# The rotary partners of the differential queries and keys, exchanged by SBUF-to-SBUF DMAs in place of TensorE's permutation products

## The reference, cut to what matters

```
q = rms_norm(x @ w_q, g_q);  k = rms_norm(x @ w_k, g_k)        # per head of 64 features
q = q * cos + partner(q) * sin;  k = k * cos + partner(k) * sin  # partner: feature d and d + 32 exchanged,
                                                               # the first half with a minus sign
p = softmax(q1 k1 / 8) - lambda * softmax(q2 k2 / 8);  out = p @ v   # 8 heads, each of two halves
```

## Time and profile before

| what | value |
|---|---|
| time, median of 3 runs | 1079.1 us (1078.55 to 1080.32) |
| time of the profiled execution | 1077.96 us |
| its span, first to last instruction | 1076.2 us |
| TensorE busy | 1042.4 us (97% of the span) |
| VectorE, ScalarE, GpSimd busy | 731.7, 552.9, 202.2 us |
| granted TensorE clock, mean | 0.995 |
| DMA: the core's queue of SyncE | 191.15 MB, 52.5% of 16 engines |
| the stretch of a slab in the queries and keys | 14.74 us |

### The profile page before, as it was taken

One profiled execution on the slowest core, in us unless ns is written; L12 is line 12 of the kernel. 1 busy time (PEld: TensorE's weight loads), 2 busy tenths in 40 slices (PEclk: granted clock), 3 DMA queues, 4 the chain that ended last, 5 costly groups with the idle time before them and its releaser, 6 DMA issues.

```text
span 1076.2 us, 20430 instructions
## 1 busy us (share of the span) xinstructions
PE 1042.4 (97%) x7993; PEld 981.9 (91%) x7993; DVE 731.7 (68%) x1155; ACT 552.9 (51%) x946; POOL 202.2 (19%) x223
## 2 busy tenths in 40 slices
PE   5999999999999999999999999999989999999998
PEld 5577788999999998989999999998877999999998
DVE  5798777767654788868556555686787765564565
ACT  2223457545363585527454444566467764544453
POOL 0000012233311001022333321021210223322010
PEclk9999999999999999999999999999999999999999
DMA  9993453577556454504564546654322265644661
GB/s 350 399 389 121 169 184 98 195 254 262 174 168 190 137 192 173 183 2 153 186 209 156 174 131 203 247 185 157 131 105 79 93 222 178 212 132 140 185 208 40
DMA packets 183587, 192.78 MB, mean 179 GB/s; under 512 B 5913, under 2 KB 143426, under 8 KB 183522
## 3 DMA queue, kind: packets, MB, share of 16 engines
q1 hardware_dynamic: 182512, 191.15, 52.5%
q0 software_dynamic: 144, 0.52, 0.2%
q10 hardware_dynamic: 866, 0.21, 0.1%
HBM read 190.83 MB, written 1.05 MB: 178 GB/s over the span
## 4 chain that ended last, share of the span: by engine, by line
PE 56%; DVE 5%; ACT 3%; issue 1%; POOL 0%; DVEq 0%; POOLq 0%; ACTq 0%
PE gemm L2219 17%; PE gemm L2221 17%; PE gemm L2220 16%; DVE wlo L1464 1%; PE aux L2717 1%; PE aux L2835 1%; PE aux L2767 1%; ACT whi L899 1%; DVE prod L1943 1%; PE gemm L2820 1%; PE aux L2773 0%; PE aux L2219 0%; DVE state L2075 0%; PE aux L2221 0%; PE aux L2220 0%
## 5 line engine op out<-in xcount | busy, mean ns | idle before, releaser
L2219 PE MATMUL gemm<-ohi,whi 128*128 128x256 f32 x1376 | 389.5, 283 | 3.8 <-issue 1.1
L1464 DVE TENSOR_TENSOR wlo<-raw,whi 128x1024 fp32r<-128x1024 f32 (+1 forms) x308 | 352.2, 1187 | 58.8 <-ACT whi L899 58.1
L2220 PE MATMUL gemm<-olo,whi 128*128 128x256 f32 x1376 | 385.8, 280 | 0.0
L2221 PE MATMUL gemm<-ohi,wlo 128*128 128x256 f32 x1376 | 383.6, 279 | 0.0
L899 ACT ACTIVATE whi<-raw 128x1024 fp32r<-128x1024 f32 (+1 forms) x308 | 276.4, 963 | 60.4 <-PE gemm L2221 44.2
L2219 PEld LDWEIGHTS gemm<-ohi,whi 128*128 128x128 f32 x1376 | 259.1, 188 | 6.7 <-DVE wlo L1464 2.8
L2220 PEld LDWEIGHTS gemm<-olo,whi 128*128 128x128 f32 x1376 | 259.5, 189 | 0.6 <-issue 0.5
L2221 PEld LDWEIGHTS gemm<-ohi,wlo 128*128 128x128 f32 x1376 | 259.4, 189 | 0.0
L2221 PE MATMUL gemm<-acthi,wlo 128*128 128x256 f32 x528 | 147.8, 280 | 0.0
L2219 PE MATMUL gemm<-acthi,whi 128*128 128x256 f32 x528 | 147.5, 279 | 0.0
L2220 PE MATMUL gemm<-actlo,whi 128*128 128x256 f32 x528 | 147.3, 279 | 0.0
(11 more groups left out here) (383 smaller groups left out, 1549.0 us busy)
## 6 DMA issues: line engine op xcount, KB each, us to landing
raw<-in_ffn_w_in SPq DMA_DIRECT2D x44, 1024.0 KB, 6.2
raw<-in_ffn_w_out SPq DMA_DIRECT2D x32, 704.0 KB, 5.2
part<-in_w_ada SPq DMA_DIRECT2D x32, 512.0 KB, 10.7
raw<-in_gla_w_in SPq DMA_DIRECT2D x6, 2048.0 KB, 7.8
raw<-in_diff_w_in SPq DMA_DIRECT2D x6, 2048.0 KB, 7.9
raw<-in_w_gate SPq DMA_DIRECT2D x11, 1024.0 KB, 6.3
raw<-in_w_up SPq DMA_DIRECT2D x11, 1024.0 KB, 8.5
raw<-in_w_down SPq DMA_DIRECT2D x16, 704.0 KB, 5.2
```

The source lines that it names most:

```text
L1464: dve.tensor_tensor(wlo[hslot][:, q * w:(q + 1) * w], src[:, q * w:(q + 1) * w], whi[hslot][:, q * w:(q + 1) * w].bitcast(F32), ALU.subtra ...
L2219: pe.matmul(dst, st_hi, mv_hi, start=start, stop=False)
L2220: pe.matmul(dst, st_hi, mv_lo, start=False, stop=False)
L2221: return pe.matmul(dst, st_lo, mv_hi, start=False, stop=stop_)
```

## The change

The `rot_d` matrix is no longer made or loaded, and the sign of the partner goes into the table `sin_d`. The partners of a pair are fetched by four DMAs of 32 partitions (32 x 2 KB, 64 KB each), which ScalarE issues: block b of 32 partitions is read from block b xor 1. They land in one of two SBUF buffers `d_rot`, which lie in the place of `ohi`. For each of the 4 DMAs the semaphore of the buffer rises by 16. ScalarE issues them for the two pairs of the stretch before in one go, in front of the third quarter (`ahead` comes before `after` at tile 0), and those of pairs 6 and 7 between the second and the third quarter of the values' slab. Before them it waits for the pair's `normalize` and, from pair 2 on, for the turn two pairs earlier. `turn` waits for the DMAs, multiplies by the sine in place and adds. The product `partners` is gone from TensorE's program, and with it the wait of `turn` for TensorE.

```
         if tag == "d":
+            sin *= rot.sum(0)[:, None]
...
+        d_t1 = sb("d_t1", 512, at=U + 10240)
+        d_rot = [sb(f"d_rot{i}", 512, at=place["ohi"] + 512 * i) for i in range(2)]
...
+            def move_partners(r):
+
+                src = tl(d_q, 2 * r, 2) if r < 4 else tl(d_k, 2 * r - 8, 2)
+                act.wait_ge(qk_normed, r + 1)
+                if r >= 2:
+                    act.wait_ge(qk_ready, r - 1)
+                for b in range(4):
+                    act.dma_start(d_rot[r % 2][32 * b:32 * b + 32, :], src[32 * (b ^ 1):32 * (b ^ 1) + 32, :]).then_inc(
+                        qk_moved[r % 2], 16)
+
             for base, name in ((0, "diff_q"), (4, "diff_k")):
                 def after(at, t, base=base):
                     buf = d_q if base == 0 else d_k
+                    if t == 0 and base + at.i:
+                        for r in (base + 2 * at.i - 2, base + 2 * at.i - 1):
+                            move_partners(r)
...
             for q in range(4):
                 ahead(*VALUES, q)
+                if q == 1:
+                    move_partners(6)
+                    move_partners(7)
             take_values(0)
...
             def turn(r):
-                me.next(qk_rot)
-                me.again(qk_ready)
-                me.did(dve.tensor_tensor(v3(d_t2[:, :], 2), v3(X[2 + r % 2][:, :], 2), bc(C("sin_d", T), 2), ALU.mult),
-                       qk_rot_read)
+                rot = d_rot[r % 2]
+                dve.wait_ge(qk_moved[r % 2], 64 * (r // 2 + 1))
+                me.did(dve.tensor_tensor(v3(rot[:, :], 2), v3(rot[:, :], 2), bc(C("sin_d", T), 2), ALU.mult), qk_turned)
                 me.next(qk_cos)
-                me.again(qk_rot_read)
-                me.did(dve.tensor_tensor(pair(r), d_t1[:, :], d_t2[:, :], ALU.add), qk_ready)
+                me.again(qk_turned)
+                me.did(dve.tensor_tensor(pair(r), d_t1[:, :], rot[:, :], ALU.add), qk_ready)
...
-            def partners(r):
-                banks.claim(X[2 + r % 2], qk_rot_read)
-                pe.wait_ge(qk_normed, r + 1)
-                src = tl(d_q, 2 * r, 2) if r < 4 else tl(d_k, 2 * r - 8, 2)
-                pe.matmul(X[2 + r % 2][:, :], C("rot_d"), src, start=True, stop=True).then_inc(qk_rot, 1)
...
-                    if t == 1 and r:
-                        partners(r - 2)
                     if t == 3:
-                        if r:
-                            partners(r - 1)
                         block_sums(r)
                         block_sums(r + 1)
...
-            value_steps(0, 8)
-            partners(6)
-            partners(7)
-            value_steps(8, 16)
+            value_steps(0, 16)
```

More of the change, by code:

```diff
@@ L77 @@
 CONSTS = [("ident", P), ("rot_q", P), ("rot_i", P), ("cos_q", T), ("sin_q", T), ("cos_i", T), ("sin_i", T),
-          ("causal", 3 * P), ("blk", P), ("rot_d", P), ("cos_d", T), ("sin_d", T), ("gla_mask", 2 * P)]
+          ("causal", 3 * P), ("blk", P), ("cos_d", T), ("sin_d", T), ("gla_mask", 2 * P)]
 COL_C, NC = column_of(CONSTS)
@@ L103, in shape_constants @@
                 cos[m], sin[m] = np.cos(ang[d % half]), np.sin(ang[d % half])
-        put("rot_" + tag, rot)
+        if tag == "d":
+            sin *= rot.sum(0)[:, None]
+        else:
+            put("rot_" + tag, rot)
         put("cos_" + tag, cos)
@@ L387, in build @@
         d_sq, d_rs = sb("d_sq", 1024, at=U + 8192), sb("d_rs", 1024, at=U + 9216)
-        d_t1, d_t2 = sb("d_t1", 512, at=U + 10240), sb("d_t2", 512, at=U + 10752)
+        d_t1 = sb("d_t1", 512, at=U + 10240)
+        d_rot = [sb(f"d_rot{i}", 512, at=place["ohi"] + 512 * i) for i in range(2)]
         d_nsq = sb("d_nsq", 2048, at=U)
@@ L452, in build @@
             sem("u_read"), sem("go_done"), sem("go_read"), sem("gated"))
-        qk_src, qk_sq, qk_stat, qk_sd, qk_normed, qk_cos, qk_rot, qk_rot_read, qk_ready = (
+        qk_src, qk_sq, qk_stat, qk_sd, qk_normed, qk_cos, qk_turned, qk_ready = (
             sem("qk_src"), sem("qk_sq"), sem("qk_stat"), sem("qk_sd"), sem("qk_normed"), sem("qk_cos"),
-            sem("qk_rot"), sem("qk_rot_read"), sem("qk_ready"))
+            sem("qk_turned"), sem("qk_ready"))
+        qk_moved = [sem("qk_moved0"), sem("qk_moved1")]
         out_done, out_read, last_read, stored = sem("out_done"), sem("out_read"), sem("last_read"), sem("stored")
```

## The result

The changed kernel takes 1082.04 us in the median of 11 runs (1080.64 to 1085.22), the kernel before in 11 runs beside it 1078.64 (1077.57 to 1080.87). The ratio is 1.0033 with a 95% interval of 1.0024 to 1.0042: 3.4 us slower by the medians, where 2.6 us faster was forecast. The range, 1074.6 to 1079.2, does not hold it. The profiled execution spans 1081.2 us against 1076.2.

The account below looks back on a forecast made before the run. TensorE was taken to bound the kernel up to pair 7's block sums, then a VectorE and GpSimd chain. 3.45 - 0.3 (issues) - 0.2 (pair 6) - 0.3 (clock) = 2.65 us, so 1079.1 becomes 1076.5; range 1074.6 to 1079.2.

Parts of the forecast that it names:

- TensorE is rid of 6.9 us, of which the pieces behind tile 3 turn into waits for the square: Eight partner products of 0.86 us leave TensorE; each of three query/key stretches gets 1.15 us shorter, 3.45 us in all.
- the cover that was forecast: In the stretches, VectorE's 1.33 us wait for tile 3 shrinks by 0.86, leaving 0.47 us to absorb lateness.
- I take 0.44 each, between, 3.5 us in all.: ScalarE's eight DMA issues a stretch, before quarter 2: quarter 2 0.3 to 0.4 us late, 0.3 us charged in total.
- Second rival: ScalarE's issues at 0.58 us make quarter 2 1.4 us late, costing 0.9 us a stretch; taken as 1078.0 us, chance 0.14.
- The DMAs land in time, 2.2 us: Partner DMAs of 64 KB land 2.2 us after issue, so everything up to pair 5 is hidden.
- The slower rival: DMAs land after 6.6 us, making turn(6) 4.0 us late and the stretches' turns 0.7; 1082.4 us, chance 0.07.
- 0.2 us charged for pair 6, nothing for pair 7: In the values, pair 6's DMAs land with 0.35 us over, less under a load's tail; pair 7's land in time.
- a gap of 1.9 us in TensorE: Before scores(1), TensorE stands from 787.5 to 789.4 waiting for take_values(0); the wait itself was taken as free.
- Clock, 0.3 charged: A clock fall in TensorE's new idle time before scores(1) would mostly use up the later 1.3 us wait; 0.3 us.
- the first rival: The clock falls in the new wait before scores(1) and lasts past 794.07: 1.7 us instead of 0.3, 1077.9 us, chance 0.18.
- Last rival: The slow clock near 805 us is absent after the shift, saving 1.7 us more: 1074.8 us, chance 0.08.
- The products of pairs 6 and 7 gain nothing: In the values, removing two products off the chain turns their 1.72 us of TensorE time into waiting.

Follow-up runs that it names:

- e1: Changed kernel with its partner DMAs issued by SyncE instead of ScalarE, in front of the following weight load; 1077.12 us, ratio 0.9988 to the kernel before.
- e6: Kernel before, all products kept, plus idle copies from ScalarE with the same bytes in 8 DMAs of 128 partitions; 1078.78 us, ratio 0.9996.
- e3: Changed kernel with TensorE's products back for pairs 0 to 5, ScalarE's DMAs only for pairs 6 and 7; 1078.09 us, ratio 1.0006.
- e9: Changed kernel with DMAs issued by SyncE, plus four unused TensorE products in front of scores(2); 1074.61 us, ratio 0.9966 to the kernel before.
- e2: Changed kernel with TensorE's products back for pairs 6 and 7, ScalarE's DMAs for pairs 0 to 5; 1080.66 us, ratio 1.0021.
- e10: Changed kernel with ScalarE's DMAs behind the fourth quarter for pairs 0 to 5, TensorE's products for pairs 6 and 7; 1075.07 us, ratio 0.9965.
- e5: Changed kernel with SyncE issuing the DMAs of pairs 0 to 5, TensorE's products for pairs 6 and 7; 1075.25 us, ratio 0.9967.
- e8: Changed kernel with ScalarE's 32 issues moved behind the fourth quarter instead of the second; 1077.13 us, ratio 0.9983 to the kernel before.
- e4: Kernel before, all products kept, plus 32 idle copies of 32 partitions issued by ScalarE at the changed kernel's places; 1081.75 us, ratio 1.0033.
- e7: Changed kernel with both pairs of a stretch in the same four DMAs, 16 issues instead of 32, from ScalarE; 1078.29 us, ratio 0.9999.

## Why the prediction was wrong, point by point

- *TensorE is rid of 6.9 us, of which the pieces behind tile 3 turn into waits for the square.* Right, once nothing else is in the way. The forecast stretch was 14.74 - 1.15 = 13.59; six versions show 13.67. In e1 VectorE waits 0.47 us for tile 3, the cover that was forecast:

```profile
763.14 0.42 DVE L2017 TENSOR_TENSOR d_k<-gemm,rstd 128x256 f32<-128x256 f32 x1 [0.47 <-PE gemm L2240]
```

- *"I take 0.44 each, between, 3.5 us in all."* **The step that failed.** An issue took 0.61 us, eight 5.0 to 6.0. The row called nearest in form, 0.49 for 128 partitions, was nearest to e6 (0.47 for 128 partitions) and not to a DMA of 32 partitions; the longest row, 0.58, would have come nearest. Quarter 2 came 1.88 us late instead of 0.35, and with 0.47 us of cover that is 1.41 of each stretch. The difference to 13.67 measured is 1.35. In the first stretch an issue of 1.47 us came on top, and the cover there was small, as forecast (0.10): quarter 2 was 2.84 us late and 2.67 were lost. The sum for the stretches was +2.16 us and not -3.1. The prediction had named issues above 0.5 us, and a clock below 1 between 788 and 800 us, as signs that it was wrong; both came.
- *Second rival, ScalarE's issues set the stretch.* The right mechanism, with its arithmetic (lateness less 0.47 of cover), but priced too low: it took 8 issues of 0.58, 4.6 us, where 5.0 to 6.0 were measured. It stood in the prediction as faster or no change; with 1.35 us lost a stretch and 2.67 in the first it crosses over.
- *The DMAs land in time, 2.2 us.* Right: 2.1 in the median. The slower rival, landing at 6.6 us, did not happen, although its 1082.4 is near the measured 1082.04; the time agreed by chance, and the turns of the stretches waited for no DMA. The 2.15 us that the prediction took from the Trainium skill ("DMA: Bandwidth & Descriptors", section "Anatomy of one DMA") is given there for DMAs that GpSimd issues; ScalarE's came out near it.
- *Values: 0.2 us charged for pair 6, nothing for pair 7.* Too low by the same term. Eight issues of 0.61 put the landing behind the turn's place and cost 0.7 us in e1 and e3. In the changed kernel one of the eight took 1.49 us, the last began at 791.70, and it was 1.52.
- *ScalarE's quarters end near 788.5 and `take_values(0)` at 789.4, which leaves a gap of 1.9 us in TensorE.* The place was right, the size not: 4.29 us, again by the issues. In e3, without the long issue, it was 3.40.
- *Clock, 0.3 charged, 1.7 as the first rival* (the text above the sum calls it the second). In the profile of the change it cost 1.69 us on the path; e9 against e1 shows 0.0022 of 1079, 2.4 us, for a wait of 3.77 us. What was held against this rival, that the new gap of 1.9 us is shorter than the one that brought a fall, is a misreading. TensorE was still at work until 802.66, and its wait before the fall was 1.91 us too:

```profile
804.57 1.78 PE L2820 MATMUL gemm<-d_k,d_q 64*128 64x256 f32 x8 [1.91 <-ACT d_p L1409]
```

That same wait of 1.91 us has a fall behind it in the kernel before, e2, e6 and e10, and none in the changed kernel and the other runs (e5 and e10 differ in this though TensorE has the same products and waits in both), and in e8 waits of 1.81 and 2.17 us passed without one. So a gap of 1.9 us can go either way. That the charge of 0.3 suits it was not tested by itself.
- *Last rival, the fall near 805 us is not there after the shift.* It was not there in the profile of the changed kernel, which took 1.7 us off the loss. As e5 and e10 show, it comes and goes without such a change, so no run ties it to this one.
- *The products of pairs 6 and 7 gain nothing.* Right, and more: e5 and e10 keep them and are the fastest versions without added work.

What stays open: why some single issues take 1.1 to 1.7 us (one in the first stretch of all eight runs that issue 32 x 2 KB DMAs there, one in the values of the changed kernel and of e4), and the mean price of the clock in the changed kernel, since each program has one profile and the mean clock of its runs differs (0.990 to 0.993).

## What to carry to other kernels

Work that leaves one engine as DMAs comes back on the issuing engine's sequencer: count the issues, multiply by a row of the same partition count, and ask what stands behind them in that engine's program. Here the same 32 issues, two quarters further down, turned a loss of 0.33% into a gain of 0.17%. And where an engine waits anyway for a chain of others, taking work from it buys only a longer wait, which can cost its clock.

## What the runs showed of the hardware

- In the three forms tried, the cost of an issue goes with the form, not with the bytes: 0.61 us for 32 partitions of 2 KB or of 4 KB, 0.47 for 128 partitions of 2 KB, on ScalarE's queue; on SyncE's 32-partition issues take 0.6 as well. Landing was 2.0 to 2.4 us in the median of each, beside weight loads; the latest single one was 4.2 us (e7).
- ScalarE's sequencer issues DMAs while earlier activations still run, so issues behind activations cost these nothing (e8). An activation behind issues waits for all of them, 3.46 us with an idle engine.
- The granted clock fell to 0.50 (1.2 GHz) during waits of TensorE of 3.77 us (e1), 4.29 (the changed kernel) and 2.88 (e7) and stayed there for about 7 us. It stayed there for about 3.5 us around the end of a wait of 3.40 us in e3 and after 1.91 us near 805 us in the kernel before. So the length of the wait alone does not say whether it falls or for how long. The Trainium skill ("TensorE: Matmul & The Clock Gate", section "HAM oscillation") warns of such gaps; e9 agrees, with 2.4 us gained by filling one.
